# Second block of a two-block network on one core: dense products of mixers a and c issued in halves between the levels of mixer b's recurrence

## The reference

```python
h = rms_norm_2(x, norm_g[l, 0]) * (1.0 + sc1) + sh1
aq, ak, av, bq, bff, bfb, bi, bg, cq, ck, cv = split(h @ w_in[l])
o_a = mixer_a(aq, ak, av)            # norm per head, rope, softmax attention, 6 heads on 2
o_b = mixer_b(bq, bff, bfb, bi, bg)  # gated recurrence, 4 heads, forward and backward
o_c = mixer_c(cq, ck, cv)            # norm per head, attention with a bias, 6 heads on 2
x = x + g1 * (concat(o_a, o_b, o_c) @ w_out[l])
x = x + g2 * conv_ffn(...)

def mixer_b(q, f_fwd, f_bwd, i, g):
    lf = log(max(lb + (1 - lb) * sigmoid(f), 1e-6))          # one for each direction
    o_f = hgrn2_scan(q, -expm1(lff), i, lff)                  # state decays by exp(lf), adds k x v
    o_b = flip(hgrn2_scan(flip(q), flip(-expm1(lfb)), flip(i), flip(lfb)))
    return rms_norm_2(o_f + o_b, g_norm) * silu(g)
```

## Time and profile before

| | us |
|---|---|
| runs: median of 3 (lowest to highest) | 3671.32 (3662.02 to 3671.84) |
| the profiled execution's own time | 3664.52 |
| its span, from first to last instruction | 3662.7 |
| PE busy | 3254.8, 89% |
| DVE, ACT, POOL busy | 1474.8, 1161.1, 1074.1 |

### The profile page before, as it was taken

The page is one execution under the profiler, slowest core; times in us unless marked ns, Lnnn a source line. Parts: engine busy times, 40 slices in busy tenths (PEclk is TensorE's granted clock), DMA queues, the critical chain, the costliest instruction groups (busy, mean ns, idle before and its releaser), DMA issues.

```text
span 3662.7 us, 44480 instructions
## 1 busy us (share of the span) xinstructions
PE 3254.8 (89%) x18015; PEld 2558.2 (70%) x18015; DVE 1474.8 (40%) x1876; ACT 1161.1 (32%) x1816; POOL 1074.1 (29%) x521
## 2 busy tenths in 40 slices
PE   5989999999997999878899768989999668989999
PEld 2866568888885775656777556667888556668887
DVE  3242337442324342444422573345430473344430
ACT  3244331212123343312223312444432312544432
POOL 0301022323341300123344222125554221125553
PEclk8998999999998999989999857999999858999999
DMA  4201016462221201165532202112333202113332
GB/s 164 55 10 37 1 35 178 126 191 75 58 64 35 54 18 24 46 207 164 164 92 69 71 1 77 30 47 87 98 94 91 59 1 77 30 47 98 96 96 91
DMA packets 440053, 279.71 MB, mean 76 GB/s; under 512 B 113466, under 2 KB 419244, under 8 KB 439468
## 3 DMA queue, kind: packets, MB, share of 16 engines
q1 hardware_dynamic: 439852, 276.87, 26.6%
HBM read 274.73 MB, written 2.10 MB: 76 GB/s over the span
## 4 chain that ended last, share of the span: by engine, by line
PE 60%; DVE 9%; issue 4%; POOL 3%; ACT 3%; DMA 2%; DVEq 0%; ACTq 0%; SPq 0%; POOLq 0%
PE ps L550 47%; POOL WL L1746 2%; PE ps L1126 2%; PE ps L990 1%; PE ps L997 1%; PE ps L1012 1%; DMA RAW<-in_w_in 1%; PE ps L1098 1%; PE ps L808 1%; DMA RAW<-in_w_ada 1%; DVE GV L1929 1%; PE ps L812 1%; ACT PR L1386 1%; DVE RSTD L1913 1%; DVE MSUM L1981 1%
## 5 line engine op out<-in xcount | busy, mean ns | idle before, releaser
L1746 POOL TENSOR_TENSOR WL<-RAW,WH 128x1024 fp32r<-128x1024 f32 (+2 forms) x366 | 860.7, 2352 | 1986.1 <-ACT WH L1310 1980.5
L550 PE MATMUL ps<-HH,WH 128*128 128x512 f32 x2504 | 878.1, 384 | 125.3 <-POOL WL L1746 75.8
L550 PE MATMUL ps<-HL,WH 128*128 128x512 f32 x2504 | 855.2, 375 | 0.0
L550 PE MATMUL ps<-HH,WL 128*128 128x512 f32 x2504 | 853.4, 375 | 0.0
L550 PEld LDWEIGHTS ps<-HH,WH 128*128 128x128 f32 x2504 | 445.1, 192 | 248.9 <-POOL WL L1746 90.7
L1310 ACT ACTIVATE WH<-RAW 128x1024 fp32r<-128x1024 f32 (+2 forms) x366 | 377.4, 1031 | 601.8 <-DMA RAW<-in_w_in 280.3
L550 PEld LDWEIGHTS ps<-HH,WL 128*128 128x128 f32 x2504 | 444.2, 192 | 85.9
L550 PEld LDWEIGHTS ps<-HL,WH 128*128 128x128 f32 x2504 | 446.6, 193 | 82.1 <-issue 1.7
L1981 DVE SCALAR_TENSOR_TENSOR MSUM<-RAW,CS,MSUM 128x1024 f32<-128x1024 f32 x140 | 210.3, 1518 | 73.2 <-DMA RAW<-in_w_ada 61.7
L1098 PE MATMUL ps<-QP,KP 64*128 64x128 f32 x640 | 79.7, 427 | 82.6 <-issue 70.2
L550 PE MATMUL ps<-FH,WH 128*128 128x512 f32 x352 | 137.0, 389 | 0.3 <-POOL WL L1746 0.3
(11 more groups left out here) (338 smaller groups left out, 4812.6 us busy)
## 6 DMA issues: line engine op xcount, KB each, us to landing
RAW<-in_w_in SPq DMA_DIRECT2D x122, 512.0 KB, 3.9
RAW<-in_w_ada SPq DMA_DIRECT2D x96, 512.0 KB, 4.3
RAW<-in_w_up SPq DMA_DIRECT2D x88, 512.0 KB, 3.8
RAW<-in_w_in SPq DMA_DIRECT2D x72, 256.0 KB, 3.7
RAW<-in_w_mod SPq DMA_DIRECT2D x32, 512.0 KB, 3.6
RAW<-in_w_down SPq DMA_DIRECT2D x32, 512.0 KB, 3.8
WMOD<-in_w_mod SPq DMA_DIRECT2D x4, 2048.0 KB, 19.2
RAW<-in_w_branch SPq DMA_DIRECT2D x16, 512.0 KB, 3.4
```

Of the source, the lines that this page charges most:

```text
L550: ins = nc.tensor.matmul(ps[0:width, t0:t0 + tn], a, b[:, k0 + k, t0:t0 + tn], start=first and k == 0 and i == 0, stop=last and k == kt - ...
L1746: nc.gpsimd.tensor_tensor(WL[s % NWS][:, 0:used], RAW[n % NRAW][:, 0:used], WH[s % NWS][:, 0:used].bitcast(F32), ALU.subtract).then_inc(*u ...
```

## The change

The second block's stages 1 to 5 are written anew; the work is the same in size, except for the points below.

- Seven units of mixer b come first: bff0, bfb0, bff1, bfb1, bg0, bg1, bq0. ACT takes the logarithms right behind the fourth, before the weights of bg1 are rounded.
- The other 13 units (bi0, bq1, bi1, then mixer a's five and mixer c's five) are issued by a generator `beside` in halves of 12 products, one after the PE work of each of the 24 items (20 levels and 4 cross blocks). Behind the first half of the next unit come the turn of the values, or the sums of squares and, for a, the rotation. The rotation is now made before the division by the root. A dense unit holds its PSUM group for two items, and the others share the remaining three.
- DD is one operation over 512 columns; four EE buffers let ACT work two items ahead. The exponentials of a level are two instructions over 256 columns. KP is made on DVE and no longer on POOL.
- Both heads' levels lie in one group of 1024 columns and are kept by one masked copy. The cross blocks are copied out by ACT. POOL clears DIAG.
- The sums with the values come once for each (t, d), by channel: weights of 128x64, two heads side by side, 128 columns moved. So nothing has to be turned, and the norm of mixer b is made as for a and c.
- Roots are taken for whole sets of heads: a's at item 21, c's and b's at the start of a's attention. The spreads for c and b (six) run between the pairs of a's attention, the spreads of a's softmax sums (three) between pairs of c's.
- The bias load moves behind the load of `w_out`'s first unit.

The core of the diff:

```diff
-            def recurrence(l):
-                for name in ("bff", "bfb"):
...
-                        for i in range(len(LEVELS)):
-                            pe.wait_ge(to_pe, at(to_pe, ("2", l, "qp", t, d, i)))
-                            pe.wait_ge(pool_out, at(pool_out, ("2", l, "kp", t, d, i)))
...
+            def beside(l):
+                before = None
+                for name, j in BESIDE:
+                    wh, wl = w_in2(l, name, j)
+                    ps = open_group(("2", l, name, j))
+                    held[0] = led.slot(("2", l, name, j))
+                    for half in range(2):
+                        if half and before:
+                            turned(l, *before)
+                        for k in range(KD // 2 * half, KD // 2 * (half + 1)):
...
+                        yield
+                    before = (name, j)
...
+            def recurrence(l):
+                for name, j in FIRST_UNITS:
+                    gemm2(l, name, j, new=None if j or name != "bff" else lambda k: ("2", l, "h", 0, k))
+                other = beside(l)
+                for s, (t, d, i) in enumerate(ITEMS):
+                    if not is_cross(s):
+                        n = level_number(s)
+                        pe.wait_ge(to_pe, at(to_pe, ("2", l, "kp", s)))
+                        qp, kp = QP[n % 2], KP[n % 2]
+                        ps = open_group(("2", l, "lev", s))
...
+                        next(other)
+                        continue
...
+                for j in range(4):
+                    pe.wait_ge(to_pe, at(to_pe, ("2", l, "inv", "a")))
+                    spread_inverse(l, "a", j, open_group(("2", l, "a", j, "spread")))
+                for _ in other:
+                    pass
```

```diff
             def open_group(key, g=None):
                 if g is None:
+                    if group[0] % 4 == held[0]:
+                        group[0] += 1
```

On DVE:

```diff
-            def decayed_queries(l, t, d, i):
...
+            def decayed(l, s):
...
+                if lv >= 2:
+                    dve.wait_ge(product_ready, at(product_ready, ("2", l, "lev", s - 2 if i >= 2 else s - 3)))
+                tiles = [EE[e] for e in e_tiles(s)]
+                V.tensor_tensor(QP[lv % 2][:, :], QH[:, t, :], tiles[0][:, :], ALU.mult).then_inc(*up(to_pe))
+                V.tensor_tensor(KP[lv % 2][:, :], KK[:, n, :], tiles[-1][:, :], ALU.mult).then_inc(
+                    *up(to_pe, ("2", l, "kp", s)))
...
+                for s, (t, d, i) in enumerate(ITEMS):
+                    if is_cross(s):
+                        keep_level(l, s - 2)
+                        cross_operands(l, s)
+                    else:
+                        decayed(l, s)
+                    if s + 2 < len(ITEMS):
+                        distances(l, s + 2)
+                    if is_cross(s):
+                        keep_level(l, s - 1)
+                    elif i >= 2:
+                        keep_level(l, s - 2)
...
+                    if s in (2 * SPAN, 2 * SPAN + 2, 2 * SPAN + 4, 2 * SPAN + 6):
+                        turn2(l, (s - 2 * SPAN) // 2)
```

More of the change, by code:

```diff
@@ L321, in program @@
[L321 to L339, removed]
@@ L507, in _ @@
         def _(pe):
-            group = [0]
+            group, held = [0], [None]
             uses = [0] * 4
@@ L937, in _, with w_in2 @@
                     break
[L940 to L943, removed]
+            def w_in2(l, name, j):
+                a = name[0]
+                if name in ("aq", "cq") and j < 3:
+                    pieces = [IN2[name] + j * 64, IN2[name] + (j + 3) * 64]
+                    loads = [("w_in_2", l * DM, KD, c, 64, P, 64 * i) for i, c in enumerate(pieces)]
+                else:
+                    col = IN2[a + "k"] if name in ("aq", "cq") else IN2[a + "v"] if name in ("avch", "cvch") else \
+                        IN2["bi"] + int(name[2]) * P if name[:2] == "bi" else IN2[name] + j * P
+                    loads = [("w_in_2", l * DM, KD, col, P, P)]
+                return take(("2", l, name, j), loads)
@@ new lines, in head_sums @@
+            def head_sums(l, a, j, ps=None, c0=0):
+                pe.wait_ge(act_out, at(act_out, ("2", l, a, j, "sq")))
+                if ps is None:
+                    ps = open_group(("2", l, a, j, "sum"))
+                x = square2_of(a, j)
+                for tb in range(NXB):
+                    ins = nc.tensor.matmul(ps[:, c0 + 2 * tb:c0 + 2 * tb + 2], x(tb), blockones[:, 0:P:64],
+                                           start=True, stop=True)
+                ins.then_inc(*up(product_ready, ("2", l, a, j, "sum")))
@@ new lines, in recurrence @@
+                        continue
+                    pe.wait_ge(to_pe, at(to_pe, ("2", l, "cross", s)))
+                    halves = [open_group(("2", l, "cross", s, h)) for h in range(2)]
+                    for n, (q, k, _, _) in enumerate(cross_blocks(d)):
+                        for h in range(2):
+                            hs = slice(64 * h, 64 * h + 64)
+                            ins = nc.tensor.matmul(halves[h][:, n * P:(n + 1) * P], k[hs, :], q[hs, :],
+                                                   start=True, stop=True)
+                            if n == 5:
+                                ins.then_inc(*up(product_ready, ("2", l, "cross", s, h)))
@@ L1697, in second_layer @@
                 recurrence(l)
-                heads2(l, "a")
-                heads2(l, "c")
+                ahead(("2", l, "wout", 0))
+                pair_attention(l, "a")
+                pair_attention(l, "c")
+                for j in range(3):
+                    high(("2", l, "mix", "c", j), XH2[:, 5 + j, :], SEQ, ("2", l, "cyN", j))
                 for m in range(KD):
@@ L2440, in recurrence @@
[L2440 to L2450 removed]
+                distances(l, 0)
@@ L2452, in second_layer @@
+                dve.wait_ge(act_out, at(act_out, ("2", l, "root", "a")))
+                V.reciprocal(HINV[:, 0:32], HSUM[:, 0:32]).then_inc(*up(to_pe, ("2", l, "inv", "a")))
+                total(l, 1)
+                for j in range(4):
+                    x = QN2["a"][:, j, :]
+                    key = ("2", l, "a", j, "spread")
+                    ps = ready(key)
+                    V.tensor_tensor(x, x, ps[:, 0:SEQ], ALU.mult).then_inc(*freed(key))
             def second_layer(l):
@@ L2454, in second_layer @@
                 recurrence(l)
-                heads2(l, "a")
-                heads2(l, "c")
+                pair_attention(l, "a")
+                dve.wait_ge(bias_in, 16 * (l + 1))
+                pair_attention(l, "c")
+                for j in range(3):
+                    key = ("2", l, "cyN", j)
+                    ps = ready(key)
+                    gv = value(("2", l, "mix", "c", j))
+                    dve.wait_ge(act_out, at(act_out, ("c", l, "sums", j)))
+                    V.tensor_tensor(gv[:, 0:SEQ], ps[:, 0:SEQ], YU2[:, j, :], ALU.mult).then_inc(*freed(key))
+                    own(key)
                 for m in range(KD):
```

807 lines of the change are left out of this document (404 added, 403 removed).

## The result

The changed kernel takes 3478.87 us (median of 4 runs, 3474.39 to 3480.23); before, on the same chip, it was 3669.72 us (4 runs). The ratio is 0.9481, with a 95% interval of 0.9465 to 0.9498. The profiled run is one of 3480.23 us with a span of 3478.4. So the gain is 191 us by the medians and 184 between the two profiled executions; the forecast was 204.

The account below looks back on a forecast made before the run. PE was taken to bound the loop, DVE nearly equal. Per layer 2.2 + 4.4 + 123.3 + 11.5 + 48.9 + 46.0 = 236.3 us, twice 472.6 against 676.4, 203.8 less: 3461 us, range 3440 to 3490.

Parts of the forecast that it names:

- The likeliest case: Dense work fills PE's waits in the second block's recurrences and the clock stays up: 3461 us, chance 0.63.
- PE's sum in the loop: PE's work in one layer's loop: halves 66.8, levels 20, cross blocks 6, values' sums 10, squares and rotations 7.0; 109.8 us.
- The waits: Waits added in the loop: weights 2.5, PSUM 5, rotations on DVE 3, clock at the start 3; 13.5 us a layer.
- The values' sums: Mixer b's sums with the values in the loop: 2.5 us each, four a layer, with an upper bound of 8.7.
- DVE: DVE's need in the loop: 80 us of operations plus 24 for 12 weight splittings on POOL, 104 us against PE's 109.8.
- the sign of long products wherever weights are split: In the loop's profile, DVE products of 2 to 2.5 us wherever POOL splits weights.
- Before the loop: PE stands 2.2 us before bg1 and 4.4 from the end of bq0; running sums covered, at most 3 us late.
- Tail and attentions: After the loop: tail 11.5 us, attention a 48.9 and attention c 46.0 in each layer.
- A port that passes on every splitting: In the loop, each weight splitting on POOL delays the keys on DVE: loop 145, 3505 us in all; chance 0.17.
- Nothing waits: The loop takes only PE's 110 us and the start 4.4: 3430 us in all; chance 0.17.
- The clock that stays low: Dense halves with waits between them also get the low clock in loop, tail and attentions: 3841 us, slower; chance 0.02.
- work that isn't moved: A missed deadline keeps the dense work on the path: 3655 to 3670 us; chance 0.01.

Follow-up runs that it names:

- Experiment 1: The changed kernel with three dense units run before the levels and the other ten behind them, none between: 3585.43 us.
- experiment 2: The changed kernel with only the sums with the values back in the older form, 128 weight columns and 64 moved: 3495.21 us.
- Experiments 8 to 10: Changed kernel, dense units whole in every second item: 3476.21 us; also rotations and `total(l, 0)` later, logarithms behind bg0's weights: 3444.22; `total(l, 0)` ending item 13: 3447.98.
- experiment 5: Changed kernel with one order altered each: `total(l, 0)` behind the next keys, 3465.73 us; just ended PSUM group passed over, 3475.23; rotations one item later, 3477.8.
- experiment 3: The changed kernel with POOL subtracting only 128 of 1024 weight columns for the 13 units in and behind the loop: 3472.19 us.
- experiment 4: The changed kernel with ACT rounding bg1's weights before the four logarithms: 3472.69 us.
- the best version: Changed kernel with whole units every second item, rotations one item later, logarithms behind bg0's weights, `total(l, 0)` last in item 13: 3447.98 us, ratio 0.9402.
- the rotations' move: The changed kernel with the four rotations one item later in DVE's order: 3477.8 us alone; with `total(l, 0)`, PSUM group and logarithms moved too: 3455.64.

## Why the prediction was right, and by how much it was off

The likeliest case came true, and its mechanism with it: the clock no longer falls in the recurrence, and dense work fills what PE waited. Experiment 1 shows the two together: without dense work between the levels PE is busy for 53.8 of 89.8 us, at 0.69 of its clock. What the clock alone is worth is shown for the sums with the values only (experiment 2). The forecast was 3461, the median is 17.9 us above it. Between the profiled executions the account is: layer 0 forecast 105.0 less, measured 95.5; layer 1 forecast 98.8, measured 93.2; 5.0 ahead of the block.

- **PE's sum in the loop (109.8, measured 118.6)** is the term that was too small, and most of the error: 8.8 us a layer, where the layers are off by 9.5 and 5.6 in all. The halves and turns were taken as 66.8 from units that follow each other, and are 73.6; the levels as 20, and are 21.8. What was left out is the change of shape, 0.1 to 0.2 us each time and 0.3 more behind a rotation. Experiments 8 to 10 get part of it back by halving the number of changes.
- **The waits (13.5, measured 11.9)** came out nearly right, and term by term in layer 0: waits at the start of a unit, for weights above all, 2.5 charged and 2.2 measured; PSUM 5 and 4.3, as waits of 1.4 us before levels 14 and 16 and before the last sum; DVE in items 12 to 18 3 and 2.1; the clock 3 and 3.2. The reason for DVE's was another: not the rotations but `total(l, 0)`, which I had charged its 0.7 us on DVE and not what is queued behind it while it waits for PE. Moving it is worth 2.1 us a layer (experiment 5). And half of the clock's share came behind that wait, not at the loop's start.
- **The values' sums (2.5, measured 2.33)** were right in size and wrong in reason: the old 0.216 a record was not the weight columns alone. Half of it was the clock (experiment 2), so the upper bound of 8.7 was one for the wrong clock; at full clock the old layout takes 4.3 to 4.5. The 2.5 rested on the attention's row of the same shape, and that held.
- **DVE (104, measured 88.4).** Without splittings it is the forecast 80 (experiment 3 has 80.03). A splitting costs 0.7 on average, not 2.0: seven of twelve begin beside masked copies or idle time and cost next to nothing, so the sign of long products wherever weights are split came true for five. Those rows stand in experiment 3, 2.04 us for an addition of 0.69 and 2.28 for a product of 0.29; and POOL's own splittings in the loop took up to 2.80 instead of 2.39, so part of the exclusion falls on POOL. The Trainium skill, "SBUF — State Buffer", section "SBUF: two separate sides", has the two engines exclude each other in both directions, and these rows agree; the 109 that I worked out by it as the most for DVE was not reached.
- **Before the loop** the gap of 2.2 (2.3) and the start of 4.4 (4.5) hold for layer 0. In layer 1 the first level came 1.6 later, the low clock behind the gap. The running sums, called covered, had 0.4 us of slack (experiment 4).
- **Tail and attentions** (11.5; 94.9): 11.7 and 96.6 in layer 0, 10.2 and 92.5 in layer 1. In layer 0 a's attention takes 50.6 (forecast 48.9), c's 45.9 (46.0).
- **The rivals.** A port that passes on every splitting (loop of 145) is refuted by experiment 3. Nothing waits (3430) fails by the 11.9 us of waits and low clock and by PE's sum. The clock that stays low and work that isn't moved did not occur: the loop's clock is 0.97.

What stays open: how the 103 us of experiment 1 divide between clock and waits; why the short gap ahead of bg1 is followed by the low clock in some layers and not in others. The loop of the best version still holds some products at the low clock at its start (it is granted 0.79 there, from 2079.9 to 2090.0), and the attentions differ between layers and runs (92.4 to 96.6 us) with the granted clock; why was not tried.

## To carry to other kernels

Dense work between the steps of a serial recurrence pays twice: it fills PE's waits, and here it kept the clock up for the small products too (a sum with the values is 4.3 us shorter by it). When pricing it, count each change of product shape, and where an operation in one engine's queue waits for another engine, ask what is queued behind it: its own duration says little (here 0.69 us of work, 7.69 of standing, 2.1 on the path). A wait that the profile puts down to one releaser may have a second close behind; the rotations' move brought nothing alone and 8.5 to 11 us a loop on top of three others, so try moves together before dropping one.

## What was not expected of the hardware

- A change of product shape on PE: the first 512-column product behind a level takes 0.34 us to the next instead of 0.23, behind a rotation 0.63; and two levels together take 1.99 where two apart take 2.18.
- The same gap ahead of a dense unit, 2.13 us of idle PE, was followed by full clock in layer 0, and in layer 1 by products at 0.43 us a record instead of 0.23, 1.6 us in all. In every kernel with that gap, that of experiment 1 aside, which has three more units there, the stretch from first gate to first level took 41.1 or 42.7 us, and in every one without it 40.6 to 40.7.
- With 64 weight columns and 128 moved a record takes 0.058 us, with 128 and 64 it takes 0.11, at the same clock.
